# The output product of a fourth layer taken one token tile after the other

## The reference, cut to what matters

```python
def window_gqa_mixer(...):                  # layers 0 and 3
    ...
    o = lax.map(block, jnp.arange(n_lat // A_BLOCK))      # softmax attention
    y_l = (o_l * jax.nn.silu(z_l)) @ w_out                # 256 x 1024 by 1024 x 1024
# first_block, at the end of each layer:
    x_lat = x_lat + gt_l[:, None, :] * rmsnorm(y_l, g_post)
# second_block, on the x_lat that comes out of layer 3:
    h = rms_norm(x, norm_mix[l])
    cols = split_columns(h @ w_in[l])
```

## Time and profile before

| | before |
|---|---|
| median of 3 runs | 1571.21 us (1568.83 to 1572.72) |
| the profiled execution's own time | 1573.01 us |
| its span in the trace | 1571.2 us |
| PE busy | 1507.2 us, 96% |
| DVE busy | 1009.9 us, 64% |
| ACT busy | 809.0 us, 51% |
| granted PE clock, mean | 0.993 |

### The profile page before, as it was taken

One profiled execution on the slowest core, in us unless ns is written; L12 is line 12 of the kernel. 1 busy time (PEld: TensorE's weight loads), 2 busy tenths in 40 slices (PEclk: granted clock), 3 DMA queues, 4 the chain that ended last, 5 costly groups with the idle time before them and its releaser, 6 DMA issues.

```text
span 1571.2 us, 28886 instructions
## 1 busy us (share of the span) xinstructions
PE 1507.2 (96%) x11163; PEld 1306.3 (83%) x11163; DVE 1009.9 (64%) x2579; ACT 809.0 (51%) x1956; POOL 111.0 (7%) x220
## 2 busy tenths in 40 slices
PE   6999999999999999999999999888999999999998
PEld 4777779977888978988999888787777799999997
DVE  3587875745655656585675799665666566566655
ACT  3566665544444454333334667654666445455543
POOL 1011110100000110010000111001101000000000
PEclk9999999999999999999999999999999999999999
DMA  9643222323322343322222442247322245555663
GB/s 357 222 129 112 95 81 88 151 84 111 114 93 84 108 151 106 118 98 95 94 98 79 178 122 82 79 136 245 106 81 69 67 147 175 173 177 169 193 198 111
DMA packets 59962, 203.41 MB, mean 129 GB/s; under 512 B 7730, under 2 KB 10498, under 8 KB 59825
## 3 DMA queue, kind: packets, MB, share of 16 engines
q1 hardware_dynamic: 58081, 197.08, 36.4%
q0 software_dynamic: 1600, 4.28, 1.4%
q10 hardware_dynamic: 144, 0.20, 0.0%
HBM read 200.43 MB, written 1.07 MB: 128 GB/s over the span
## 4 chain that ended last, share of the span: by engine, by line
PE 79%; DVE 11%; ACT 4%; issue 3%; DMA 1%; SPq 1%; POOL 1%; DVEq 0%; ACTq 0%
PE ps L48 74%; PE ps L51 5%; DVE s_wlo L57 2%; ACT SF L54 2%; DVE SF L60 1%; DVE SF L57 1%; DVE SF L75 1%; DVE SF L66 1%; DVE s_SR L57 1%; DMA s_raw<-in_weights_dram 1%; SPq L87 1%; ACT s_whi L54 1%; DMA SF<-in_weights_dram 1%; POOL s_st L57 1%; DVE s_SR L66 1%
## 5 line engine op out<-in xcount | busy, mean ns | idle before, releaser
L57 DVE TENSOR_TENSOR s_wlo<-s_raw,s_whi 128x512 fp32r<-128x512 f32 (+1 forms) x490 | 316.6, 681 | 118.8 <-ACT s_whi L54 117.5
L48 PE MATMUL ps<-s_Hh,s_whi 128*128 128x256 f32 (+2 forms) x992 | 322.9, 326 | 1.5 <-DVE s_Hl L57 1.5
L48 PE MATMUL ps<-s_Hh,s_wlo 128*128 128x256 f32 (+2 forms) x992 | 312.1, 315 | 0.0
L48 PE MATMUL ps<-s_Hl,s_whi 128*128 128x256 f32 (+2 forms) x992 | 311.9, 314 | 0.0
L54 ACT ACTIVATE s_whi<-s_raw 128x512 fp32r<-128x512 f32 (+1 forms) x490 | 281.6, 620 | 52.7 <-PE ps L48 47.9
L54 ACT ACTIVATE SF<-ps 128x512 f32<-128x512 f32 (+3 forms) x328 | 146.8, 464 | 252.6 <-PE ps L51 165.2
L48 PEld LDWEIGHTS ps<-s_Hh,s_whi 128*128 128x128 f32 (+1 forms) x992 | 187.6, 189 | 28.5 <-issue 16.3
L48 PE MATMUL ps<-s_whi,s_Hh 128*128 128x256 f32 (+1 forms) x688 | 208.4, 303 | 0.9 <-DVE s_Hl L66 0.7
L48 PEld LDWEIGHTS ps<-s_Hh,s_wlo 128*128 128x128 f32 (+1 forms) x992 | 187.8, 189 | 13.2
L48 PE MATMUL ps<-SF 128*64 128x128 f32 (+6 forms) x1368 | 191.2, 311 | 6.4 <-DVE SF L60 4.2
L48 PEld LDWEIGHTS ps<-s_Hl,s_whi 128*128 128x128 f32 (+1 forms) x992 | 188.0, 189 | 10.7
(11 more groups left out here) (198 smaller groups left out, 2575.1 us busy)
## 6 DMA issues: line engine op xcount, KB each, us to landing
s_raw<-in_weights_dram SPq DMA_DIRECT2D x308, 512.0 KB, 4.2
GF<-in_weights_dram SPq DMA_DIRECT2D x32, 512.0 KB, 9.0
SF<-in_weights_dram SPq DMA_DIRECT2D x16, 512.0 KB, 12.0
s_raw<-in_weights_dram SPq DMA_DIRECT2D x6, 384.0 KB, 3.6
s_gp<-in_l_g_post_dram POOLq DMA_DIRECT2D x16, 128.0 KB, 3.8
s_bg<-in_l_b_ada_dram POOLq DMA_DIRECT2D x16, 128.0 KB, 4.6
SF<-ext_rows SPq DMA_DIRECT2D x16, 128.0 KB, 3.2
s_X<-in_ctx_dram SPq DMA_DIRECT2D x2, 512.0 KB, 5.0
```

What stands on the lines that cost most here:

```text
L48: return self.e.matmul(*a, **k)
L57: return self.e.tensor_tensor(*a, **k)
```

## The change

The fourth layer's output products are taken tile by tile: TILES, pairs (j, i): (0,0), (1,0), (3,0), (2,0), (0,1), (1,1), (3,1), (2,1). The jobs come in the order 0, 1, 3, 2. Jobs 3 and 2 are both placed in SR now. Job 3 lies where the attention's keys were (SR 0 to 4095) and waits for the last score alone, so that it is cast in slots 36 and 37 of the attention, two pieces a slot beside the units. Job 2 is cast as the first thing behind the attention. The early chunks are 26 in place of 21, of the products (0,0), (1,0), (0,1) and (3,0), in an order by k. p 512 and p 768 go into the rings, p 1024 into SR after the product (3,1). Banks, waits and the places of the norm's steps follow. DVE's calls of `dve_cast` in `v_layer_a` and `v_out` are changed as ACT's in `act_layer_a` and `act_out`, which the diff below shows.

```diff
 def plan():
-        jobs += mix(l) + [job(("out", l, j), f"l{l}_w_out", 256 * j, 256) for j in range(4)]
+        jobs += mix(l) + [job(("out", l, j), f"l{l}_w_out", 256 * j, 256) for j in (range(4) if l < 3 else (0, 1, 3, 2))]
...
-OUT_SEQ = (BOTH, BOTH, BOTH, LONE)
+
+TILES = [(LAT, j, i) for j, i in ((0, 0), (1, 0), (3, 0), (2, 0), (0, 1), (1, 1), (3, 1), (2, 1))]
+OUT_SEQ = (BOTH, BOTH, BOTH, TILES)
...
-        placed["p", 512] = two(self.SR[:, 7168:11264]) + (self.mixer_done(3),)
+        placed["out", 3, 3] = two(self.SR[:, 0:4096]) + ([("score", UNIT_AT[4])],)
+        placed["out", 3, 2] = two(self.SR[:, 7168:11264]) + (self.mixer_done(3),)
+        placed["p", 1024] = two(self.SR[:, 0:4096]) + ([("out", 55)],)
...
     def out_bank(self, l, n):
+        if l == 3:
+            return (7, 6, 0, 5, 3, 6, 4, 5)[n]
...
     def out_early(self, l):
         ns = range(len(OUT_PRE[l]))
+        if l == 3:
+            some = [(n, k) for k in range(5) for n in (0, 1)] + [(4, k) for k in range(5)]
+            return some + [(0, 5), (1, 5)] + [(2, k) for k in range(6)] + [(n, 6) for n in ns]
         return [(n, k) for n in ns for k in range(6)] + [(n, 6) for n in ns if l != 2]
...
-                self.pe_turn_2(pe, 0, 16, True, (0, 1, 2, 3), (("row_max", 128), ("row_max", 128), ("prob_ev", 128), ("ysq", 51)))
+                self.pe_turn_2(pe, 0, 16, True, (0, 1, 2, 3), (("ysq", 51), ("row_max", 128), ("prob_ev", 128), ("ysq", 53)))
...
+        if l == 3:
+            return (("q_ev", Q_AT[3] + 8), ("vec", 2), ("row_max", UNIT_AT[4]), ("gf", GF_AT[4] - 1), ("z", ZZ_AT[3] + 8), ("ysq", at + 2),
+                    ("gf", GF_AT[4]), ("ysq", at + 4))[n]
...
-            self.act_cast(act, min(w.first(("q", l, 0)) + 4 * slot // per + 5, w.end(("out", l, 1))))
+            self.act_cast(act, min(w.first(("q", l, 0)) + 4 * slot // per + 5 + (max(0, slot - 35) if l == 3 else 0), w.end(("out", l, 1 if l == 0 else 3))))
...
     def act_out(self, act, l):
+        if l == 3:
+            self.act_cast(act, w.end(("out", l, 2)))
...
-            if n == (3 if l < 3 else 0):
+            if n == 3 and l < 3:
                 self.act_cast(act, w.end(("out", l, 2)))
-            if n == (4 if l < 3 else 1):
+            if n == 4 and l < 3:
                 self.act_cast(act, w.end(("out", l, 3)))
...
     def act_out_3(self, act, n):
-        if n == 2:
+        if n == 4:
+            self.act_square_2(act, 0, 12, self.F(11264, 2, D))
             self.act_cast(act, w.end(("p", 512)))
         if n == 5:
-            self.act_square_2(act, 0, 12, self.F(11264, 2, D))
+            self.act_h_2(act, 0, 32, (0, 1, 2, 3), 0)
             self.act_cast(act, w.end(("p", 768)))
-        if n == 6:
-            self.act_h_2(act, 0, 32, (0, 1, 2, 3), 0)
...
     def v_out_3(self, v, n):
-        if n == 2:
-            self.dve_cast(v, w.end(("p", 512)))
+        if n == 3:
+            self.m0 = self.v_out_mean(v, 3, LAT, 0)
         if n == 4:
-            self.m0 = self.v_out_mean(v, 3, LAT, 0)
+            self.v_x_new(v, 3, LAT, 0, self.m0)
         if n == 5:
-            self.v_x_new(v, 3, LAT, 0, self.m0)
             mean = self.v_mean_2(v, 17)
             self.v_xn_2(v, 0, mean, tiles)
+            self.dve_cast(v, w.end(("p", 512)))
+            self.v_h_2(v, 0, 32, (0, 1, 2, 3), 0)
+        if n == 6:
+            self.dve_cast(v, w.first(("p", 768)) + 2)
+        if n == 7:
             self.dve_cast(v, w.end(("p", 768)))
-        if n == 6:
-            self.v_h_2(v, 0, 32, (0, 1, 2, 3), 0)
-        if n == 7:
             m = self.v_out_mean(v, 3, LAT, 1)
+            self.dve_cast(v, w.first(("p", 1024)) + 2)
             self.v_x_new(v, 3, LAT, 1, m)
             self.dve_cast(v, w.end(("p", 1024)))
             mean = self.v_mean_2(v, 18)
```

More of the change, by code:

```diff
@@ L921, in bank_free @@
             return "ysq", at + n - 3
-        if l in (0, 3):
-            return (("q_ev", Q_AT[l] + 8), ("ada_dst", 16) if l == 0 else ("vec", 2), ("z", ZZ_AT[l] + 8), ("gf", GF_AT[l + 1]), ("ysq", at + 1),
+        if l == 3:
+            return (("q_ev", Q_AT[3] + 8), ("vec", 2), ("row_max", UNIT_AT[4]), ("gf", GF_AT[4] - 1), ("z", ZZ_AT[3] + 8), ("ysq", at + 2),
+                    ("gf", GF_AT[4]), ("ysq", at + 4))[n]
+        if l == 0:
+            return (("q_ev", Q_AT[l] + 8), ("ada_dst", 16), ("z", ZZ_AT[l] + 8), ("gf", GF_AT[l + 1]), ("ysq", at + 1),
                     ("ysq", at + 2), ("ysq", at + 4), ("gf", GF_AT[l + 1] - 1))[n]
@@ L1453, in v_layer_a @@
                                        self.z_tile(l, t0)[:, 256 * (s0 if l == 0 else 0):][:, 0:256], op0=ALU.mult, op1=ALU.mult).then_inc(S["gf"], 1)
-            self.dve_cast(v, min(w.first(("q", l, 0)) + 4 * slot // per + 5, w.end(("out", l, 1))))
+            self.dve_cast(v, min(w.first(("q", l, 0)) + 4 * slot // per + 5 + (max(0, slot - 35) if l == 3 else 0), w.end(("out", l, 1 if l == 0 else 3))))
             if j == per // 2 + 1 and t < 8:
@@ L1514, in v_out @@
         w = self.w
+        if l == 3:
+            self.dve_cast(v, w.end(("out", l, 2)))
         for n in range(len(OUT_SEQ[l])):
```

## The result

The changed kernel takes 1562.47 us, median of 5 runs (1559.68 to 1565.26), for 1571.21 before (1568.83 to 1573.11, also 5 runs); the ratio on record is 0.9928, 95% interval 0.990 to 0.9955. The quotient of the two medians is 0.9944, inside that interval. The profiled execution is that median, with a span of 1560.7 us. The page's line of engines, to be held against the earlier trace rows: PE has lost 5.0 us of busy time with the same 11163 instructions.

What follows compares the result with a forecast made beforehand. PE bounds the kernel, but layer 3's output stage goes at the pace of casting jobs 2, 3 and p 512. -8.6 + 0.2 + 0.2 = -8.2 takes 1571.2 to 1563.0 us; 8 in 10 range 1559.5 to 1567.0.

Steps and rivals of the forecast that it cites:

- Output stage: Layer 3's output stage, from the last s_Gl to the second block: 14.7 us for 23.3, a gain of 8.6.
- The margin of 0.5 at tile 0's turn: Output stage: the norm ends at 10.5 and PE comes to the transposes at 11.0, so no wait, by only 0.5.
- The attention's end: End of the attention: five more early chunks cost 1.8, filling an s_Gl wait saves 1.6, small stops cancel: +0.2 us.
- cover of 2.2 on DVE: Attention, slot 37: the last unit's normalising is done at 1011.7, wanted at 1013.9, so job 3's casts were taken as 0.
- The stop of 0.2 expected in slot 33: Attention, slot 33: PE waits 0.2 and a restart for a low part that product (1,0)'s chunk wants from DVE.
- Tile 1: Tile 1's turn: DVE's list ends at 23.6, PE arrives at 23.4, so a wait of about 0.2 us is added.
- Transfers: Loads for jobs 2, 3 and p 1024: nothing is held, cost 0, with a bound of 5.7 us late.
- Behind it: From tile 1's transposes on PE's list is the same, so all of the shift arrives at the end unless the clock changes.
- The 3.3 us of low clock: From 1063.3 to 1110 the granted clock of 0.93 costs 3.3 us; the same cost was taken after the change.
- rival 3: Stretch behind 1063: the clock meets another phase, -3.3 us or about +1.7 each, 1559.7 or 1564.7; chance 0.15.
- Sum: Whole kernel: -8.6 + 0.2 + 0.2 = -8.2 us, from the median of 1571.2 to 1563.0.

## Why the prediction was right, point by point

- *Output stage, -8.6.* 23.30 before, 14.51 after (1018.69 to 1033.20), -8.8. No stop inside, as said. The margin of 0.5 at tile 0's turn is there: the normed tile ends at 1028.97, the turn is at 1029.50. The cause was right for this arrangement (casts ahead of the norm: put back, they cost 2.64 at once), but too simple for the old one, where the norm alone brings nothing. The count of casts leaves out that DVE and ACT wait for each other between the old groups. That is most of the gain: DVE's idle time up to tile 1's turn was 9.85 us before and is 3.87 now.
- *The attention's end, +0.2.* +0.33 from the mark (the last s_Gl ends at 1018.64 for 1018.10 before, and 0.2 of that arose ahead of the mark). The reason was half wrong, so that the size came out nearly right is in part luck: it is made up of +1.53 for the five chunks, -1.48 for their order and +0.28 for the casts. The five more chunks fill nothing; the wait for s_Gl goes because of their order. Taking the chunks by step removes it without a price that shows, and without the five further chunks step 7 comes 1.2 earlier than before (21.32 for 22.52). The casts, put at 0, cost about 0.28, and their cover of 2.2 on DVE wasn't the one that ends first: ACT's is about 1. The stop of 0.2 expected in slot 33 doesn't show as one.
- *Tile 1, +0.2.* 8.82 for 8.68, so 0.14; DVE's list was the bound, as counted, by little: it is done 0.05 before PE's transposes begin. That it would swallow further gains ahead of it I had not drawn from it.
- *Transfers, 0.* No wait for a load up to tile 1's turn; SP's 16 issues begin at 1047.05, 8.03 earlier, which is PE's shift (8.12 at tile 1's turn) within 0.1.
- *Behind it.* I wrote that all of the shift arrives and nothing else. The profiled pair says 2.4 more. The 3.3 us of low clock were 0.04 x 46.8 = 1.9 this time. That is rival 3 in part, and as I see it now it isn't a branch that the change takes but the spread of every execution.
- *Sum.* -8.2 predicted, -8.3 to tile 1's turn, -8.7 between the medians. The large term was right and for the most part for its reason; that the small ones hit as well is partly chance, as the two points on the attention's end and on the stretch behind show.

## What to carry to other kernels

When a stage has several chains of nearly equal length, count each engine's whole list up to the point where PE stands alone again, not only the first chain: fillers, earlier norms and saved waits here came to nothing one by one, because DVE's list up to tile 1's norm was the next bound. Then look at the idle time inside that list: 6.0 of the 8.3 us came with the same 46 instructions on DVE, mostly because it no longer waits for ACT between groups of casts, and 2.3 with four casts fewer. Two parts of a change that both shorten the same chain (6.0 and 7.3 here) don't add up (8.3). And where a difference of a microsecond is to be read, set a mark in the trace ahead of the change and one behind it: the change was the same to 0.01 us there in two executions, while nearly the same code behind it took from 517 to 530 us.

## What the runs showed of the hardware

- *The clock falls in one execution and not in another at the same stops.* The kernel before and the one with p 512 behind the norm have the same PE instructions and the same two stops up to there (1.43 and 1.65 us; it fell about as the second began). The first stayed at the full level; PE's stretches of the second:

```profile
1014.00:1018.00 4.00, 1.95 (x21) 0.95 0.02 4
1018.00:1022.00 4.00, 2.97 (x14) 0.50 0.26 87
1022.00:1026.00 4.00, 4.00 (x26) 0.69 0.83 265
```

  0.50 is the level of 1.2 GHz throughout. The Trainium skill (TensorE: Matmul & The Clock Gate, "What's actually happening") has the chip watch PE in a rhythm of its own, which doesn't start with the kernel. The two traces agree with that, since equal stops met different clocks; the rhythm itself no trace here shows.
- *A low clock costs nothing where something else is late.* In the kernel before with its early chunks by step, the clock was low in the four us from 1014 and the four from 1018 (0.72 and 0.85), and still tile 0's turn stands 18.85 behind step 7, to the hundredth as before: the low clock cost 0.28 x 4 + 0.15 x 4 = 1.7 us, and the stops of 0.79 for s_SR and 0.51 for a bank with their restarts, which the kernel before has there, are missing in this trace. Behind tile 0's turn, where PE isn't kept waiting, the same trace has 0.72 from 1034 to 1038, and the way to tile 1's turn is 13.88 us for 13.13.
- *The landing that ends the wait for s_Gh varies by itself*: 8.74, 7.54, 8.17, 9.13, 7.95, 7.41 us in the first six traces, behind the same 16 transfers, and 7.54 and 7.81 in the two executions of the changed kernel.
